# Hybrid decoder layer with 32 experts: gates and the output's initial rows made tile by tile within the projection, bias words in the attention, pass table behind the positions

## The reference

```
h = h + y @ w_out
xt = rms_norm(h, g_ffn)
logits = xt @ w_router + b_router
top_vals, top_idx = top_k(logits, 4);  gates = softmax(top_vals)
for each expert e and the rows that chose it:
    a  = clamped_swiglu(row @ w1[e] + b1[e])
    out[row] += gate * (a @ w2[e] + b2[e])
```

## Time and profile before

| | before |
|---|---|
| median of 3 runs | 2165.1 us (2160.9 to 2166.31) |
| the profiled execution | 2162.8 us |
| its span in the trace | 2161.1 us |
| PE busy in the span | 2080.2 us (96%) |
| DVE busy | 1477.3 us (68%) |
| ACT busy | 1192.9 us (55%) |
| POOL busy | 212.2 us (10%) |
| PE's share of the chain that ended last | 71% |

### The profile page before, as it was taken

The page is one execution under the profiler, slowest core; times in us unless marked ns, Lnnn a source line. Parts: engine busy times, 40 slices in busy tenths (PEclk is TensorE's granted clock), DMA queues, the critical chain, the costliest instruction groups (busy, mean ns, idle before and its releaser), DMA issues.

```text
span 2161.1 us, 35581 instructions
## 1 busy us (share of the span) xinstructions
PE 2080.2 (96%) x11530; PEld 1681.5 (78%) x11531; DVE 1477.3 (68%) x2291; ACT 1192.9 (55%) x1651; POOL 212.2 (10%) x201
## 2 busy tenths in 40 slices
PE   6999989988999999999999999999999999999997
PEld 4443678866799778877979797977779979888895
DVE  3251486668866787688676767678986666567666
ACT  3241375246645676567564646477764555555545
POOL 2000300012101111011010101011010110101001
PEclk9999999989999999999999999999999999999999
DMA  7000302118966699689686868679996677668556
GB/s 269 1 0 6 144 27 88 40 55 321 357 227 207 231 340 355 194 324 358 232 275 240 268 234 262 231 258 368 336 373 212 194 242 273 185 206 297 188 197 219
DMA packets 203128, 477.39 MB, mean 221 GB/s; under 512 B 14743, under 2 KB 20951, under 8 KB 203024
## 3 DMA queue, kind: packets, MB, share of 16 engines
q1 hardware_dynamic: 185598, 437.69, 55.9%
q0 software_dynamic: 17424, 39.17, 7.5%
q10 hardware_dynamic: 66, 0.02, 0.0%
HBM read 468.99 MB, written 32.11 MB: 232 GB/s over the span
## 4 chain that ended last, share of the span: by engine, by line
PE 71%; DVE 10%; issue 7%; DMA 6%; ACT 4%; DVEq 1%; ACTq 1%; POOLq 1%; SPq 0%; POOL 0%
PE ps L1288 16%; PE ps L1290 16%; PE ps L1289 16%; PE ps L1023 8%; DVE w_lo L1842 4%; DMA out<-y,idx_cur 4%; PE ps L1401 2%; DMA ring<-in_w 1%; PE ps L1168 1%; PE ps L1170 1%; PE ps L1169 1%; PE ps L1282 1%; ACT ring L719 1%; DMA xh<-in_x 1%; DVE xT L1842 1%
## 5 line engine op out<-in xcount | busy, mean ns | idle before, releaser
L890 ACT ACTIVATE w_hi<-ring 128x1024 fp32r<-128x1024 f32 x730 | 781.7, 1121 | 422.1 <-PE ps L1290 370.0
L1842 DVE TENSOR_TENSOR w_lo<-ring,w_hi 128x1024 fp32r<-128x1024 f32 x732 | 862.3, 1220 | 188.3 <-ACT w_hi L890 188.3
L1288 PE MATMUL ps<-xT,w_hi 128*128 128x256 f32 x1248 | 354.2, 284 | 0.0
L1290 PE MATMUL ps<-xT,w_lo 128*128 128x256 f32 x1248 | 353.1, 283 | 0.0
L1289 PE MATMUL ps<-xT,w_hi 128*128 128x256 f32 x1248 | 353.1, 283 | 0.0
L1288 PE MATMUL ps<-w_hi,xT 128*128 128x512 f32 x816 | 323.3, 396 | 13.2 <-issue 6.9
L1289 PE MATMUL ps<-w_lo,xT 128*128 128x512 f32 x816 | 319.5, 392 | 0.0
L1290 PE MATMUL ps<-w_hi,xT 128*128 128x512 f32 x816 | 319.5, 391 | 0.0
L1288 PE MATMUL ps<-w_hi,actT 128*128 128x512 f32 x644 | 262.8, 408 | 0.0
L1290 PE MATMUL ps<-w_hi,actT 128*128 128x512 f32 x644 | 251.6, 391 | 0.0
L1289 PE MATMUL ps<-w_lo,actT 128*128 128x512 f32 x644 | 251.1, 390 | 0.0
(11 more groups left out here) (312 smaller groups left out, 2400.7 us busy)
## 6 DMA issues: line engine op xcount, KB each, us to landing
ring<-in_w SPq DMA_DIRECT2D x390, 1024.0 KB, 7.2
xh<-in_x SPq DMA_DIRECT2D x4, 2048.0 KB, 16.1
work<-in_w_out SPq DMA_DIRECT2D x1, 4096.0 KB, 12.9
token_rows<-uT POOLq DMA_DIRECT2D x8, 512.0 KB, 2.9
out<-xh SPq DMA_DIRECT2D x8, 512.0 KB, 9.1
work<-in_w_in SPq DMA_DIRECT2D x2, 1536.0 KB, 18.0
uT<-in_w_mem_kv SPq DMA_DIRECT2D x1, 2048.0 KB, 14.5
ring<-in_w_in SPq DMA_DIRECT2D x1, 1536.0 KB, 16.9
```

The lines of the kernel that those rows point to most:

```text
L890: act_e.activation(hi, raw, ACT.Copy).then_inc(hi_ready, counted(h, whole))
L1288: pe.matmul(acc, hi, whi, start=first, stop=False, skip_group_check=shared)
L1290: return pe.matmul(acc, lo, whi, start=False, stop=last, skip_group_check=shared)
L1842: return dve.tensor_tensor(lo, x, hi.bitcast(F32), ALU.subtract)
```

## The change

Three things move.

1. **Gates and initial rows into the projection.** For tiles 0 to 5 the exponential, the gates, their words, their transposes and the two half rows of the output are made within the projection, two or three tiles behind the chunks. A gate needs an exponential and the norm needs a square root, so ACT loads the table of the one and of the other in each tile. The product of a half row (`init_product`) goes through PSUM bank 6, which is also the bank of `turn_row`; so the first `turn_row` of a tile now also waits (`init_d`) until DVE has taken the half row out of it. Two half rows of tile i-3 are added by DVE within `residual(i)`. All 16 half rows are now finished on DVE, none on ACT.
2. **b2's words into the attention.** The three transfers of b2 (32x1024, three copies) are issued right behind the load of `W_out`, and ACT makes their high words in items 1, 2 and the zero words in item 3, DVE the low words in item 3.
3. **The passage is put in another order.** Half rows of tile 5 and the plus one on b1 come before the last tile's logits, b1's transposes before the positions, the pass table directly behind the positions, and the half rows of tiles 6 and 7 behind the table. The stores of the finished rows of tiles 0 to 4 are issued within the projection.

The core of the diff (buffer names and unchanged helpers left out):

```diff
@@ SP
+            for k in range(3):
+                sp.dma_start(b2_raw[k * E:(k + 1) * E, :], b2[0]).then_inc(b2_in, 16)
...
+            for t in range(last_gates - 1):
+                store_rows(t)
             sp.wait_ge(b1_zero, 1)
@@ ACT, attention
+                if j == 1:
+                    act_e.wait_ge(b2_in, 48)
+                    act_e.wait_ge(ylru, LT)
+                    act_e.activation(b2_top, b2_raw[2 * E:3 * E, :], ACT.Copy).then_inc(b2_hi, 1)
+                elif j == 2:
+                    act_e.activation(b2_r[0:2 * E, :], b2_raw[0:2 * E, :], ACT.Copy).then_inc(b2_hi, 1)
+                elif j == 3:
+                    for a, n in ((b2_r[3 * E:P, :].rearrange("p (a b) -> p a b", b=P), KD), (gatesT_r[3 * E:P, :, :], 2)):
...
@@ ACT, projection
             for i in range(NT):
+                if i >= 2:
+                    exponentials(i - 2)
+                    act_e.preload_act_table(ACT.Sqrt)
                 if i + 1 < NT:
                     row_hi(i + 1, 0)
                 if i:
                     take_turned(i - 1)
                 if i + 1 < NT:
                     row_hi(i + 1, 1)
+                if i >= 2:
+                    gate_hi((i - 2,))
+                if i + 1 < NT:
                     row_hi(i + 1, 2)
+                if i >= 2:
+                    take_gates((i - 2,))
@@ PE, projection
             def turn_row(i, m2):
                 if m2 == 0:
                     pe.wait_ge(xr_ready, i + 1)
                 if 2 * i + m2:
                     pe.wait_ge(xt_out, 2 * i + m2)
+                if i >= 2 and m2 == 0:
+                    pe.wait_ge(init_d, 2 * min(i - 2, last_gates - 2) + (1 if i < NT - 1 else 2))
...
             for i in range(1, NT):
                 for n in range(6):
                     chunk(i, n)
-                    if n in (2, 3):
+                    if n == 0 and i >= 3:
+                        init_product(i - 3, 0)
+                    elif n in (2, 3):
                         turn_row(i - 1, n - 2)
                     elif n == 4:
                         route_logits(i - 1)
+                        if i >= 3:
+                            init_product(i - 3, 1)
+                    elif n == 5 and i >= 2:
+                        turn_gates(i - 2, 0)
@@ DVE, projection
+            def init_rows(t, half):
+                dve.wait_ge(init_mm, 2 * t + half + 1)
+                hh = xh[:, t, half * HALF:(half + 1) * HALF]
+                dve.tensor_tensor(hh, ps[:, init_bank(t, half), :], hh, ALU.add).then_inc(init_d, 1)
 
             def residual(i):
...
+                        if g == 0 and half == 0 and i >= 3:
+                            init_rows(i - 3, 0)
+                        elif g == 2 and half == 0 and i >= 2:
+                            gate_lo(i - 2, i - 1)
+                            if i >= 3:
+                                init_rows(i - 3, 1)
                     if i + 1 < NT:
                         row_lo(i + 1, g)
+                    if g == 1 and i >= 2:
+                        gates_of(i - 2, i - 1)
@@ DVE, passage
+            for half in range(2):
+                init_rows(last_gates - 1, half)
+            dve.wait_ge(b1_in, 32)
+            odd = b1_raw[0:2 * E, :].rearrange("p (n two) -> p two n", two=2)[:, 1, :]
+            dve.tensor_scalar(odd, odd, 1.0, None, ALU.add).then_inc(b1_plus, 1)
+            take_logits(NT - 1)
+            choose(NT - 1)
+            gates_of(last_gates, NT)
...
             dve.tensor_copy(ttab[0:1, 0:3 * P], ps[0:1, 2, 0:3 * P]).then_inc(ttab_ready, 1)
 
+            for t in (last_gates, NT - 1):
+                for half in range(2):
+                    init_rows(t, half)
             dve.wait_ge(ttab_ready, 1)
```

More of the change, by code:

```diff
@@ L159, in hymba_layer @@
         gate_w = sb_early("gate_w", [P, 2, LT, P])
-        lru_words = sb_early("lru_words", [P, 2, LT, P], F32R)
+        gatesT_r = sb_early("gatesT_r", [P, 2, P], F32R)
+        with ExitStack() as below:
+            lru_words = below.enter_context(nc.sbuf_tensor("lru_words", [P, 2, LT, P], F32R))
+        table_tmp = sb_early("table_tmp", [P, 2 * LT * P])
         w_rt = sb_early("w_rt", [P, KD, E])
@@ L200, in hymba_layer @@
         early.close()
[L201 to L204, removed]
         with ExitStack() as between:
@@ L304, in unit_bank, with init_bank @@
             return i % 4 if units[i][1] != V else 6 + units[i][0]
[L306 to L318, removed]
+        last_gates = NT - 2
+        def init_bank(t, half):
+            return 6 if t < last_gates - 1 else 4 + half if t == last_gates else half
         normt = [(uT[:, K, :], S, C_KS), (km[:, :, :].rearrange("p a b -> p (a b)"), 2 * MEM, C_KM)]
@@ L446, in _, with store_rows @@
                 load_slot(0, s)
-            sp.wait_ge(op_done, 6 * NT)
-            for k in range(3):
-                sp.dma_start(b2_sb[k * E:(k + 1) * E, :], b2[0]).then_inc(b2_in, 16)
+            def store_rows(t):
+                sp.wait_ge(init_d, 2 * t + 2)
+                sp.dma_start(out[0, t * P:(t + 1) * P, :], xh[:, t, :]).then_inc(init_out, 16)
+            for t in range(last_gates - 1):
+                store_rows(t)
             sp.wait_ge(b1_zero, 1)
@@ L453, in _ @@
             sp.wait_ge(ttab_ready, 1)
+            sp.wait_ge(init_d, 2 * NT)
             for s in range(4, RAW):
                 load_slot(0, s)
[L456 to L460, removed]
+            for t in range(last_gates - 1, NT):
+                store_rows(t)
             total = sp.value_load(ttab[0:1, TALL:TALL + 1], min_val=1, max_val=NPASS)
@@ L865, in _ @@
                              b1_raw.rearrange("p (j c two) -> p j two c", j=4, two=2), ACT.Copy).then_inc(b1_hi, 1)
+            first_hi(4)
             first_hi(5)
-            for i in range(EARLY_A, NA):
-                init_rows(i)
             act_e.wait_ge(ttab_ready, 1)
@@ L1239, in _ @@
             pe.wait_ge(op_out, 6 * NT)
-            def init_product(kind, n):
-                if kind == "a" and n >= EARLY_A:
-                    pe.wait_ge(init_a, n - EARLY_A + 1)
-                    init_row(n)
-                if kind == "d" and n >= 2:
-                    pe.wait_ge(init_d, n - 1)
-                i, cols = init_half(kind, n)
-                pe.matmul(ps[:, init_bank(kind, n), :], gatesT_r[:, i * P:(i + 1) * P], b2_r[:, cols],
-                          start=kind == "d", stop=True).then_inc(init_mm, 1)
+            pe.wait_ge(b1_plus, 1)
+            for i in range(2 * KD):
+                m = pe.transpose(ps[:, 3, i * E:(i + 1) * E],
+                                 b1_raw[0:E, (i // 2) * 2 * P:(i // 2 + 1) * 2 * P].rearrange("p (c two) -> p two c", two=2)[:, i % 2, :],
+                                 ident[0:E, 0:E])
+            m.then_inc(b1_turned, 1)
             pe.wait_ge(mask_ready, NT)
@@ L1750, in _ @@
             link(dve.memset(cmask[:, 0, :], 0.0))
-            for i in range(NT + 1):
-                if i < NT:
-                    residual(i)
-                    ffn_norm(i)
+            for i in range(NT):
+                residual(i)
+                ffn_norm(i)
                 if i >= 1:
@@ L1855, in _ @@
             take_xlo(1, 0, 6)
-            for n in range(1, len(init_halves["d"])):
-                init_rows(n)
             dve.wait_ge(b1_hi, 2)
```

178 lines of the change are left out of this document (90 added, 88 removed).

## The result

The changed kernel takes 2179.97 us (median of 6 runs, 2177.26 to 2180.66) against 2164.31 before (6 runs, 2160.9 to 2169.88): a ratio of 1.0069 (95% interval 1.0058 to 1.0080), 15.7 us slower. The profiled execution took 2180.16 with a span of 2178.4, 17.3 longer than that of before.

A forecast was written before the change was run, and what follows sets the result against it. PE was taken to set the projection's pace; 10.4 (projection) + 3.9 (attention) - 6.1 (passage) = +8.2 on 2165.1 gave 2173.3 us. The forecast's own range was 2168 to 2179, the one-in-ten range 2163.5 to 2180.5.

The forecast's parts named there:

- Projection, +10.4: Projection, tiles 3 to 7: PE's turn 1.77 later for DVE's half row, plus a 0.3 product, five times: +10.4 us.
- PE does not wait at the turn: Rival, projection: half row done when PE arrives, a tile pays only PE's own 0.75; 2166.7 us, chance 0.16.
- DVE becomes the bound: Rival, projection: DVE's added 2.3 us outgrow its waiting, 1.5 more a tile, +7.5; 2180.8 us, chance 0.10.
- Table loads hidden: Projection: ACT's two table loads a tile, 2.56, and 0.8 of small operations lie in its 4.34 wait; cost nothing.
- Attention, +3.9: Attention, items 1 and 3: ACT 3.05 late from b2's wait and words, 1.3 behind item 3; nine tenths arrive: +3.9 us.
- So 0.95 of 1.05 arrives: Attention: claimed nine tenths of ACT's delay behind an odd item reaches the end, read from items 2 to 5.
- starting in another clock: Loop of passes, taken as untouched: its starting in another clock would upset the whole forecast; no size given.
- Passage, -6.1: Passage to the first b1 product: half rows, low words and gates saved, less later logits: 6.1 us earlier.
- The 0.9 of the later logits: Passage: the last tile's logits taken 0.9 us later, because the plus one on b1 waits for its transfers.
- PE's start: Passage: PE's products before the first b1 product begin 7.6 us earlier; if they decide, the passage gives back 7.6.
- Sum, +8.2: Whole kernel: 10.4 + 3.9 - 6.1 = +8.2 us, median 2173.3 us.
- The tables are on the path: Rival, projection: table loads do not hide, 12 x 1.28 = 15.4 us more; 2188.7 us, chance 0.04.

The follow-up runs named there:

- Run 3: Changed kernel with both half rows of tile i-3 placed behind the logits, so no turn waits for DVE: 2171.88 us, ratio 1.0028.
- run 7: Changed kernel with b2's transfers ahead of W_out, no turn waiting for DVE, and 12 more table loads on ACT: 2171.32 us, ratio 1.0034.
- run 1: Changed kernel with b2's three transfers issued ahead of the W_out load, all operations where they were: 2172.19 us, ratio 1.0037.
- Run 4: Kernel before with one added wait, no work: ACT waits behind item 1 of the attention for the g_ffn load: 2168.55 us, ratio 1.0017.
- Run 9: Changed kernel, b2's transfers first, no turn waiting for DVE, b2's words in the projection, two low words on POOL instead of four: 2160.39 us, ratio 0.9982.
- run 2: Changed kernel with b2's transfers ahead of W_out and b2's words moved behind even items 2, 4 and 6: 2174.41 us, ratio 1.0037.
- Run 6: Changed kernel with b2's transfers first, no turn waiting for DVE, and POOL's four low words directly behind the gather: 2174.68 us, ratio 1.0044.

## Why the prediction was right and where it was off

The direction was right, and so was the largest reason given for it: slower, for the new wait of PE's turn on DVE. The second reason, the attention, had its price wrong. By its steps:

- **Projection, +10.4**: measured +10.8. The idle (1.33 against 1.3), the tile (15.96 against 15.9) and the five tiles came as worked out. Run 3 shows that the wait was the cause and not DVE's added work. The rivals "PE does not wait at the turn" and "DVE becomes the bound" are refuted.
- **Table loads hidden**: right, and run 7 gives the price beyond the cover, 4.7 for twelve.
- **Attention, +3.9**: measured +13.1 in the profiled execution; this is the step that failed. "So 0.95 of 1.05 arrives" held for the work (2.5 in run 1, where 2.2 was expected), and b2's landing was right to 0.3. But the wait was priced as ACT's lateness alone, as though PE behind it kept its clock. It did not: 2.7 of waiting became 10.7, the difference to run 1 (7.8 between the medians). Run 4 shows a fall of the clock behind a wait with no work at all. The second fall, at 338, has no wait ahead of it that a run ties it to; run 3's trace, with the wait and without that second fall, has 6.3 in place of 13.1. The text named a loop "starting in another clock" as what would upset the whole; it was the attention.
- **Passage, -6.1**: measured -4.7. The 0.9 of the later logits was right (1.03). "PE's start" was better than thought (10.9 earlier against 7.6), and `sel` became the last, as written, but came 4.1 earlier, not 5.5. DVE's low words ahead of it were taken at their old duration, and they had a neighbour now: 6.69 against 2.36, 4.3 more. It was partly repaid, because the 2.05 that DVE needed to enter the loop before now ran beside the stalled instructions. Run 9, with POOL out of their way, has them at 1.2 each. The operations that the change left alone were the ones to check.
- **Sum, +8.2**: measured +15.7 between the medians, nearly twice as much. That 2179.97 lies inside 2163.5 to 2180.5, by half a microsecond, is luck: the upper end had been put there for "DVE becomes the projection's bound" and "The tables are on the path", and neither happened. The forecast's own range does not hold it, and its 2179 does not follow from the three terms either: their upper bounds add up to 10.4 + 4.4 - 4.5 = +10.3, or 2175.4. The attention's term was a third of what it measured. Its excess of 9.2 is the whole miss of the profiled execution (17.3 against 8.2); what the other stretches missed by cancels out.

## What to carry to other kernels

When a change lets one engine wait in front of PE, price what the wait does to PE's clock, not only the lateness: here 1.92 without any work cost 6.1 in one execution and 3.4 in the median. When work is taken out of a stretch, look which operations now meet that used to follow one another; here they were DVE's and POOL's. And a wait that a buffer's reuse brings (here PSUM bank 6) can be mended by the order alone: here the same instructions, placed later, gave 7.9 of 10.8 back.

## What the runs showed of the hardware that I had not expected

- The granted clock of PE fell to 1.2 GHz behind an idle of 4.28, 2.39 and 1.89 (the changed kernel, runs 4 and 2), and not behind one of 1.88 in run 1. It is not a matter of that one idle alone. In run 9 it was low at 274 to 278, where its attention is that of before and the idle ahead is 1.60; in the trace of before, an idle of 1.61 at the same place left it at 1.00. Run 6's trace has a fall at the same place behind 1.61. Run 9, PE's timeline, and the view by windows:

```profile
273.08 2.79 PE L1148 MATMUL ps<-vm,ring 128*128 128x64 f32 x16 [1.60 <-ACT ring L727]
```

```profile
274.00:276.00 2.00, 2.00 (x12) 2.00 (x12) 0.10 (x1) 2.00 (x10) 0.00 (x0) 0.52 1.05 422
```

  The second fall in the changed kernel, at 338, has no idle over 0.76 in the 20 us ahead of it. What sets it off stays open.
- A DVE instruction of 0.19 took 10.18 beside POOL (run 6): the whole run of four POOL instructions went by before it ended, not just the one that was under way. Why POOL kept its turn four times there, and alternated with DVE in the changed kernel (6.69 for DVE's two, 12.57 for POOL's four), no run here tells.
